# Taking x by quarters in the value product of a gated-MLP layer, with one x chunk turned on VectorE

## The chip, the core and the metric

The program runs on one core of a Trainium2 chip: TensorE (PE) multiplies, VectorE (DVE) and ScalarE (ACT) work elementwise, GpSimd (POOL) does little here, and SyncE (SP) issues the transfers that bring weights from memory. The metric is the device time of one execution in microseconds (us).

## What is computed

A two-layer encoder over 256 tokens of 2048 features, in float32. Layer 0 has the even mixer (spatial gating beside pooling), layer 1 an attention mixer; each is followed by a convolutional feed-forward block. The change lies in the beginning of the even mixer:

```python
h = rms_norm(x, norm_mix_g[i])
p = h @ w_in_even[e]                                  # 2048 -> 3072 columns: u, v, pool
z = jax.nn.gelu(p[..., :2 * A_WIDTH], approximate=False)
...
v = group_layer_norm(v, ln_g, ln_b)                   # v: columns 1024 to 2047 of p
w = jnp.where(block_causal_mask(A_BLOCK)[None], w_s, 0)
gate = jnp.einsum('gts,bnsgd->bntgd', w, v) + b_s...
y_a = u * gate
```

## The kernel before

**Pieces.** All weights come in pieces of 1 MB (128 partitions x 2048 floats), through a ring of four places (`RING`). SP issues the loads in a fixed order; the load of piece c waits until piece c - 4 has been split (`s_low`). ACT writes the rounded high part of a piece (`high`, L445), DVE the remainder (`low`, L821), and PE multiplies with both. `high` and `low` of piece c also wait until PE is through with piece c - 4 (`s_used`).

**Quads.** The values v are the first product: pieces 0 to 7, each a "quad" of four blocks of 128 features by 512 columns. A quad is 16 matmuls with the high part and 8 with the low part (`straight_quad`, L1369; `first_quad`, L1422 and L1427, for piece 0), and its sums stay in a PSUM bank pair of psA for its column half c. Before, column half 0 runs over the four quarters q of the features first (pieces 0 to 3), then column half 1 (pieces 4 to 7).

**Turning x.** The products need x with features on the partitions. x is taken in four chunks of 512 features. PE transposes a chunk against an identity (`transpose_x`, L1399, 8 matmuls) into PSUM; ACT multiplies by the gain and rounds (`turned_high`, L483, 4 instructions), DVE writes the remainder (`turned_low`, L845, 4 instructions), and then `s_turned` lets PE use the chunk. For the other norms DVE can do the turning instead (`turn_blocks`, L863: 16 block transposes into `xT`).

**The order of the work.** Each engine has one instruction stream, written by hand. On ACT and DVE, after a short prologue, a loop over n holds `high(n + 3)` or `low(n + 3)` and beside it what is listed for that n; what is behind a waiting instruction waits with it. Here "step n" is such a turn of the loop, and "quad n" is PE's n-th quad.

**Beside the quads.** ACT sums squares of x (`squares`), DVE makes 1/rms of each token (`mean_square`, `rstd_columns`, with ACT's `root` between them) and spreads it over rows (`spread_rstd`, L902). PE transposes small vectors, the taps of the convolutions and the spatial weights after quad 3 (L1452 to L1461). DVE copies them out (`spatial_weights`, L923 to L927) and signals `s_WT`. After quad 6 PE waits for `s_WT` and sums the spatial weights with a matmul against ones (L1465) into bank 0 of psT. DVE copies that sum (L998) and signals `s_wsr`, on which PE waits before the first pool product (`turned_half`, L1330), since that one writes banks 0 and 1 of psT. ACT's `gelu_v` (L517) reads the finished column halves from psA, at steps 3 and 7.

The order of PE around the quads, before:

```python
for c in range(2):
    for q in range(4):
        n = N_V0 + 4 * c + q
...
pe.wait_ge(s_wsr, 1)
```

Of the kernel before, what the change touches and what calls it, by code (L numbers as in the profile page):

```python
# [29 lines left out]
P = 128  # L30
RING = 4
LEAD = 3
# [17 lines left out]
def build(nc, x_in, norm_mix_g, norm_ffn_g, final_norm_g, w_in_even, ln_v_g, ln_v_b, w_spatial,  # L50
# [9 lines left out]
    AG = ln_v_g.shape[1]  # L60
# [4 lines left out]
    N_V0 = 0  # L65
# [35 lines left out]
    with ExitStack() as ctx:  # L101
# [169 lines left out]
        def turned_bank(s, n, kk):  # L271


            if s in (1, 3):
                return xT[n][:, kk, :]
            return psT[:, 2 * (n % 2) + kk // 2, TOK * (kk % 2):TOK * (kk % 2) + TOK]

        block = ctx.enter_context(nc.Block())
# [3 lines left out]
        def _(sp):  # L282
# [5 lines left out]
                sp.dma_start(raw[:, c % RING, :].rearrange("p (k n) -> p k n", k=kk), src)\  # L288
                    .then_inc(s_raw[c % RING], 16)

            for c in range(2):
                for q in range(4):
                    if c == 0 and q == 0:
                        piece0 = raw[:, 0, :].rearrange("p (k n) -> p k n", k=4)
                        src = quad(W_IN0, 0, 2)
                        sp.dma_start(x[:, :, 0:256], X_IN[:, :, 0:256]).then_inc(s_x_a, 16)
                        sp.dma_start(x[:, :, 256:512], X_IN[:, :, 256:512]).then_inc(s_x[0], 16)
                        sp.dma_start(piece0[:, 0:2, :], src[:, 0:2, :]).then_inc(s_raw_a, 16)
                        sp.dma_start(piece0[:, 2:4, :], src[:, 2:4, :]).then_inc(s_raw[0], 16)
                        continue  # L300
                    if c == 0:
                        sp.dma_start(x[:, :, 512 * q:512 * q + 512], X_IN[:, :, 512 * q:512 * q + 512])\
                            .then_inc(s_x[q], 16)
                    load(N_V0 + 4 * c + q, quad(W_IN0, q, 2 + c))
                if c == 0:

                    sp.dma_start(rows[32:64, :], norm_ffn_g.rearrange("l (m p) -> (l m) p", p=P)).then_inc(s_rows, 16)
                    sp.dma_start(rows[64:72, :], pool_scale[0].rearrange("(m p) -> m p", p=P)).then_inc(s_rows, 16)
                    sp.dma_start(rows[72:80, :], ln_v_g[0].rearrange("g (m p) -> (g m) p", p=P)).then_inc(s_rows, 16)
                    sp.dma_start(rows[80:88, :], ln_v_b[0].rearrange("g (m p) -> (g m) p", p=P)).then_inc(s_rows, 16)  # L310
                    for l in range(2):
                        sp.dma_start(conv_rows[:, l, 0:3, :], conv_w[l].rearrange("j (m p) -> m j p", p=P)).then_inc(s_conv, 16)
                        sp.dma_start(conv_rows[:, l, 3, :], conv_b[l].rearrange("(m p) -> m p", p=P)).then_inc(s_conv, 16)
                    sp.dma_start(w_sp, w_spatial[0].rearrange("g t s -> t g s")).then_inc(s_sp, 16)
                    sp.dma_start(bs, b_spatial[0:1, :, :].to_broadcast([P, AG, P])).then_inc(s_bs, 16)
            for j in range(4):
                for k in range(2):
                    load(N_POOL + 2 * j + k, half(W_IN0, k, 2 * AW + 256 * j))
# [106 lines left out]
        def _(a):  # L425
# [74 lines left out]
            a.wait_ge(s_raw[0], 16)  # L500
            a.activation(wh[:, 0, PIECE // 2:], raw[:, 0, PIECE // 2:], ACT.Copy).then_inc(s_high, 1)
            squares(0, 0)
            for n in range(1, 4):
                turned_high(0, n)
                if n < LEAD:
                    high(n)


            def gelu_v(c):

                a.wait_ge(s_used, N_V0 + 4 * c + 4)
                if c == 0:
                    a.wait_ge(s_rstd, 1)
                for t in range(2):
                    for g in range(2):
                        i = 4 * t + 2 * c + g
                        ins = a.activation(z[:, t, 512 * c + GD * g:512 * c + GD * g + GD],  # L517
                                           psA[:, 2 * c + t, GD * g:GD * g + GD], ACT.Gelu,
                                           scale=rstd[:, t:t + 1], accum_out=vsum[:, i:i + 1])
                fenced(ins, s_z, c + 1)  # L520
# [32 lines left out]
            for n in range(N_OUT0 + 16):  # L553
                k = n - N_OUT0
                if k in (6, 10, 14):
                    turned_high(1, k // 4 - 1)
                high(n + LEAD)
                if n < 2:
                    squares(0, n + 1)
                if n == 1:  # L560
                    squares(0, 3)
                if n == 1:
                    root(0)
                if n in (3, 7):
                    gelu_v(n // 4)
                if n in (8, 9):
                    z_squares(n - 8)
                if n == 10:
                    a.wait_ge(s_var, 1)
                    fenced(a.activation(vsd, vvar, ACT.Sqrt), s_zsd, 1)  # L570
                if N_POOL <= n < N_POOL + 8 and n % 2:
                    copy_low_half(Q_POOL + n // 2 - 4, (n // 2) % 2, n)
                if N_POOL + 2 <= n <= N_POOL + 8 and n % 2 == 0:
                    pooled_high(n // 2 - 5)
                if n == N_U[0][1]:
                    copy_low_half(Q_U[0], 0, n)
                if n in (N_WPOOL - 1, N_WPOOL):
                    for j in (0, 1) if n < N_WPOOL else (2, 3):
                        if j < 3:
                            a.wait_ge(s_wp, j + 1)  # L580
                        copy_low_half(Q_WPOOL + j, 0, n if j == 3 else None, bank=2 * (j % 2))
                    for j in (0, 1) if n < N_WPOOL else (2, 3):
                        yb_high(j)
                if n - 1 in N_GATE:
                    ya_high(N_GATE.index(n - 1))
                if n in N_GATE:
                    j = N_GATE.index(n)
                    if j:
                        copy_low_half(Q_U[j], j % 2, N_U[j][1])
                    gelu_u(j)  # L590
                if k >= 4 and k % 4 == 0:
                    squares(1, k // 4 - 1)
# [208 lines left out]
        def _(ve):  # L801
# [52 lines left out]

            def turn_blocks(s, n, tokens):


                for i in tokens:
                    for j in range(4):
                        src = x[32 * i:32 * i + 32, :, 512 * n:512 * n + 512]\  # L860
                            .rearrange("p t (k j b) -> p t k j b", k=4, j=4)[:, :, :, j, :]
                        dst = xT[n][32 * j:32 * j + 32, :, :].rearrange("p k (t i b) -> p t k i b", t=2, i=4)[:, :, :, i, :]
                        ins = ve.transpose(dst, src)  # L863
                if 3 in tokens:
                    ins.then_inc(s_turn, 1)
# [43 lines left out]

            ve.wait_ge(s_vec, 1)  # L910
            fenced(ve.tensor_copy(cols[:, 0:32], psA[:, 2, 0:32]), s_cols, 1)
            for n in range(4):
                turned_low(0, n)
                if n < LEAD:
                    low(n)

            def spatial_weights():

# [65 lines left out]
            for n in range(N_OUT0 + 16):  # L984
                k = n - N_OUT0
                if k in (6, 10, 14):
                    turned_low(1, k // 4 - 1)
                low(n + LEAD)
                if n == 1:
                    mean_square(0)  # L990
                    rstd_columns(0)
                if n == 4:
                    spatial_weights()
                if n == 5:
                    spread_rstd()
                if n == 6:
                    ve.wait_ge(s_wsum, 1)
                    fenced(ve.tensor_copy(WTsum, psT[:, 0, :].rearrange("p (g t) -> p g t", g=AG)), s_wsr, 1)  # L998
                    link(ve.memset(pp[:, :, 0:16], 0.0))
                    ve.wait_ge(s_bs, 16)  # L1000
                if n == 8:
# [306 lines left out]
        def _(pe):  # L1308
# [99 lines left out]
            def first_quad():  # L1408
# [3 lines left out]
                for kk in range(4):  # L1412
# [1 line left out]
                        pe.wait_ge(s_turned_a, 1)  # L1414
                        pe.wait_ge(s_high_a, 1)
                    if kk == 2:
                        transpose_x(0, 1)
                        pe.wait_ge(s_turned, 1)
                        pe.wait_ge(s_high, 1)
                    for t in range(2):  # L1420
# [14 lines left out]
            warm(5)  # L1435


            for c in range(2):
                for q in range(4):
                    n = N_V0 + 4 * c + q  # L1440
                    if n == 0:
                        first_quad()
                    else:
                        if c == 0:
                            pe.wait_ge(s_turned, q + 1)
                        straight_quad(n, c, H, 4 * q, q == 0, q == 3)
                    if n in (0, 1):
                        transpose_x(0, n + 2)
                    if n == 3:

                        pe.wait_ge(s_rows, 16 * 4)
                        pe.transpose(psT[:, 2, 8 * FT:8 * FT + 88], rows, ident[0:88, 0:88])  # L1452
# [9 lines left out]
                        ins.then_inc(s_spT, 1)  # L1462
                    if n == 6:
                        pe.wait_ge(s_WT, 1)
                        pe.matmul(psT[:, 0, :], ones[:, :], WT.rearrange("p g t -> p (g t)"), start=True, stop=True)\  # L1465
                            .then_inc(s_wsum, 1)
            pe.wait_ge(s_wsr, 1)
            for j in range(4):
                for k in range(2):
                    if j >= 2 and k == 0:  # L1470
                        pe.wait_ge(s_added, Q_POOL + j - 1)
                    turned_half(N_POOL + 2 * j + k, k, j % 2, H)
# [232 lines left out]
```

## Time and profile before

| | us |
|---|---|
| median of 3 runs | 2091.39 (2091.25 to 2091.41) |
| profiled execution, its own time | 2091.88 |
| span of the profiled execution | 2090.2 |
| PE busy | 2077.9 |
| DVE busy | 1577.1 |
| ACT busy | 1051.6 |

The time outside the span is 1.7 us. Times in the text count from the span's start. A matmul's duration in the trace overlaps its successor's, so the pace of PE is read from the starts of the weight loads (PEld), one for each matmul.

### The profile page before, as it was taken

To read this page: it belongs to the slowest core of one execution; us is meant where nothing else is said; L and a number is where in the kernel's file an instruction comes from. 1 tells how busy PE (TensorE), PEld (TensorE's weight loads), DVE (VectorE), ACT (ScalarE), POOL (GpSimd) and SP (SyncE) were. 2 spreads that over 40 slices of the span, in tenths; PEclk is the share of its full clock that TensorE was granted. 3 is DMA by queue.
4 is the path that set the end of the run, shared out by engine and by line. 5 is a ranking of instruction groups with operands and counts; after the bars stand their busy time and mean duration, and the time that the engine had idled before them with its cause. 6 is when DMAs were issued, how large, how long until landed. Compare 5 with 4: busy or idle time off the path is not lost.

```text
span 2090.2 us, 29731 instructions
## 1 busy us (share of the span) xinstructions
PE 2077.9 (99%) x10934; PEld 1793.5 (86%) x10934; DVE 1577.1 (75%) x2005; ACT 1051.6 (50%) x1095; POOL 25.4 (1%) x57
## 2 busy tenths in 40 slices
PE   9999999999999999999999999999999999999998
PEld 7888888888888888888888888888888888888886
DVE  6888886777676776776787788997776677767677
ACT  7554564445444444455554554465454444444454
POOL 0000000000000000000010000000000000000000
PEclk9999999999999999999999999999999999999999
DMA  8645565555555655554665565556555556556552
GB/s 300 201 164 200 181 204 199 182 200 182 192 191 182 208 190 181 195 190 147 204 206 163 191 208 175 175 184 212 195 185 189 194 184 204 181 181 200 181 198 105
DMA packets 317188, 397.17 MB, mean 190 GB/s; under 512 B 8612, under 2 KB 240844, under 8 KB 317004
## 3 DMA queue, kind: packets, MB, share of 16 engines
q1 hardware_dynamic: 313500, 391.27, 56.0%
q0 software_dynamic: 1056, 3.16, 0.8%
q10 hardware_dynamic: 2576, 1.98, 0.3%
q8 instruction: 36, 0.59, 0.1%
q14 instruction: 20, 0.16, 0.0%
HBM read 394.28 MB, written 2.11 MB: 190 GB/s over the span
## 4 chain that ended last, share of the span: by engine, by line
PE 96%; DVE 1%; SPq 1%; issue 1%; ACT 1%; DMA 0%; DVEq 0%; ACTq 0%
PE ps_turned L1330 37%; PE ps_straight L1369 33%; PE ps_turned L1339 20%; PE ps_straight L1330 1%; PE ps_turned L1369 1%; PE ps_straight L1339 1%; DVE w_low L821 0%; DMA w_raw<-in_w_in_even 0%; PE ps_straight L1604 0%; ACT w_high L445 0%; PE ps_straight L1614 0%; SPq L288 0%; PE ps_straight L1489 0%; PE ps_straight L1624 0%; PE ps_turned L1565 0%
## 5 line engine op out<-in xcount | busy, mean ns | idle before, releaser
L821 DVE TENSOR_TENSOR w_low<-w_raw,w_high 128x2048 fp32r<-128x2048 f32 x369 | 844.6, 2292 | 348.0 <-ACT w_high L445 314.1
L445 ACT ACTIVATE w_high<-w_raw 128x2048 fp32r<-128x2048 f32 x368 | 704.0, 1917 | 662.2 <-PE ps_straight L1369 286.7
L1330 PE MATMUL ps_turned<-h_split,w_high 128*128 128x512 f32 x3456 | 802.8, 390 | 0.9 <-DVE work L998 0.9
L1330 PEld LDWEIGHTS ps_turned<-h_split,w_high 128*128 128x128 f32 x3456 | 643.6, 188 | 131.8 <-DVE work L998 1.3
L1339 PEld LDWEIGHTS ps_turned<-h_split,w_low 128*128 128x128 f32 x3456 | 425.1, 192 | 6.1 <-DVE w_low L821 0.2
L1339 PE MATMUL ps_turned<-h_split,w_low 128*128 128x256 f32 x3456 | 428.9, 283 | 0.0
L1369 PE MATMUL ps_straight<-w_high,y_split 128*128 128x512 f32 x1792 | 425.5, 390 | 0.4 <-DVE x L872 0.4
L1369 PEld LDWEIGHTS ps_straight<-w_high,y_split 128*128 128x128 f32 x1792 | 335.9, 188 | 70.3 <-issue 0.8
L1369 PE MATMUL ps_straight<-w_low,y_split 128*128 128x512 f32 x896 | 221.3, 389 | 0.0
L1369 PEld LDWEIGHTS ps_straight<-w_low,y_split 128*128 128x128 f32 x896 | 168.2, 188 | 34.9
L1058 DVE SCALAR_TENSOR_TENSOR work<-work,conv_columns 128x256 f32<-128x256 f32 x352 | 154.4, 480 | 12.2 <-DVE work L1058 2.5
L872 DVE TENSOR_TENSOR x<-x,ps_straight 128x512 f32<-128x512 f32 x182 | 116.7, 682 | 54.4 <-PE ps_straight L1369 53.6
L603 ACT ACTIVATE work<-work,conv_columns 128x256 f32<-128x256 f32 x176 | 95.6, 590 | 60.0 <-DVE work L831 59.9
L454 ACT ACTIVATE work<-ps_turned 128x512 f32<-128x512 f32 x108 | 64.7, 599 | 92.8 <-PE ps_turned L1330 78.5
L827 DVE TENSOR_TENSOR work<-ps_turned,work 128x512 f32<-128x512 f32 x108 | 74.4, 689 | 27.9 <-ACT work L454 25.1
L1369 PE MATMUL ps_straight<-w_high,h_split 128*128 128x512 f32 x368 | 90.0, 397 | 0.0
L1369 PEld LDWEIGHTS ps_straight<-w_high,h_split 128*128 128x128 f32 x368 | 68.3, 188 | 14.2 <-issue 0.5
L1190 DVE STREAM_TRANSPOSE work<-work 32x96 f32<-32x96 f32 x256 | 69.1, 270 | 13.1 <-DVE small L1178 7.9
L831 DVE TENSOR_TENSOR work<-work,rstd_rows 128x512 f32<-128x512 f32 x103 | 71.3, 692 | 3.5
L863 DVE STREAM_TRANSPOSE work<-x 32x256 f32<-32x256 f32 x128 | 55.8, 436 | 2.0
L1369 PE MATMUL ps_straight<-w_low,h_split 128*128 128x512 f32 x184 | 45.5, 390 | 0.0
L1369 PEld LDWEIGHTS ps_straight<-w_low,h_split 128*128 128x128 f32 x184 | 34.5, 188 | 7.2
(186 smaller groups left out, 756.1 us busy)
## 6 DMA issues: line engine op xcount, KB each, us to landing
w_raw<-in_w_up SPq DMA_DIRECT2D x176, 1024.0 KB, 5.0
w_raw<-in_w_down SPq DMA_DIRECT2D x88, 1024.0 KB, 5.0
w_raw<-in_w_in_odd SPq DMA_DIRECT2D x48, 1024.0 KB, 5.5
w_raw<-in_w_in_even SPq DMA_DIRECT2D x23, 1024.0 KB, 5.3
w_raw<-in_w_out_even SPq DMA_DIRECT2D x16, 1024.0 KB, 4.9
w_raw<-in_w_out_odd SPq DMA_DIRECT2D x16, 1024.0 KB, 5.0
work<-c_rows POOLq DMA_DIRECT2D x8, 256.0 KB, 6.5
x<-in_x SPq DMA_DIRECT2D x3, 512.0 KB, 11.1
```

Of the source, the lines that this page charges most:

```text
L445: a.activation(wh[:, s, :], raw[:, s, :], ACT.Copy).then_inc(s_high, 1)
L454: fenced(a.activation(spare, src, ACT.Copy), s_spare, at(q + 1, 4, r))
L603: ins = a.activation(cc[j % 2][:, m, :], up[:, m, 2:], ACT.Identity, scale=taps[:, l, 2, bass.ds(i, 1)], bias=taps[:, l, 3, bass.ds(i, 1)])
L821: ve.tensor_tensor(wl[:, s, :], raw[:, s, :], wh[:, s, :].bitcast(F32), ALU.subtract).then_inc(s_low, 1)
L827: fenced(ve.tensor_tensor(to, src, spare, ALU.add), s_added, at(q + 1, 4, r))
L831: return ve.tensor_tensor(ap, ap, factor.unsqueeze(1).to_broadcast([P, 2, TOK]), ALU.mult)
L872: ins = ve.tensor_tensor(xc, xc, psA[:, 2 * (i % 2) + t, :] if sums is None else sums[:, t, :], ALU.add)
L1058: ins = ve.scalar_tensor_tensor(out=c[:, m, :], in0=up[:, m, 2 - back:TOK + 2 - back], scalar=taps[:, l, 2 - back, bass.ds(i, 1)], in1=c[: ...
L1190: ins = ve.transpose(dst, src)
L1330: ins = pe.matmul(ps[:, 2 * slot + m, :], hi[:, kk, P * m:P * m + P], acts[:, K, :], start=(K == 0 and not narrow_ran), stop=(K == KC - 1) ...
L1339: ins = pe.matmul(ps[:, 2 * slot + m, TOK:], lo[:, kk, P * m:P * m + P], acts[:, K, 0:TOK], start=(K == 0 and opens), stop=(K == KC - 1), ...
L1369: return pe.matmul(ps[:, 2 * slot + t, :], acts[:, k0 + kk, a0:a0 + P], weights[:, kk, :], start=begin, stop=end)
```

## The change

The eight quads run in another order: both column halves of a feature quarter one after the other (q outside, c inside), so that quad n uses x chunk n // 2. The loads follow: piece 1 comes before x chunk 1, and piece 3 before x chunk 3. Of x, PE transposes chunk 1 after quad 0 (it stood in the middle of quad 0) and chunk 2 after quad 2; chunk 3 is transposed by DVE in two halves, in steps 0 and 1, into `xT[0]`, and ACT and DVE split it in step 2. `squares(0, n + 1)` and `root` go with it to steps 0 to 2 and 3. DVE's `spread_rstd` moves from step 5 to 4, `spatial_weights` from 4 to 5, the copy of the spatial sums from 6 to 7; PE's small transposes move from behind quad 3 to behind quad 4. `gelu_v` moves to steps 6 and 7. The spatial sums go to bank 3 of psT, and PE waits for their copy ahead of the second pool panel (`j == 1`) instead of the first.

```diff
@@ SyncE
-            for c in range(2):
-                for q in range(4):
...
+            for q in range(1, 4):
+                if q == 1:
+                    load(N_V0 + 1, quad(W_IN0, 0, 3))
+                sp.dma_start(x[:, :, 512 * q:512 * q + 512], X_IN[:, :, 512 * q:512 * q + 512]).then_inc(s_x[q], 16)
+                if q < 3:
+                    load(N_V0 + 1 + q, quad(W_IN0, 1, 1 + q))
...
+            for q in (2, 3):
+                for c in range(2):
+                    load(N_V0 + 2 * q + c, quad(W_IN0, q, 2 + c))
@@ ScalarE
-            for n in range(1, 4):
+            for n in range(1, 3):
+                high(n)
                 turned_high(0, n)
-                if n < LEAD:
-                    high(n)
...
-                a.wait_ge(s_used, N_V0 + 4 * c + 4)
+                a.wait_ge(s_used, N_V0 + 7 + c)
...
                 high(n + LEAD)
-                if n < 2:
+                if n < 3:
                     squares(0, n + 1)
-                if n == 1:
-                    squares(0, 3)
-                if n == 1:
+                if n == 3:
                     root(0)
-                if n in (3, 7):
-                    gelu_v(n // 4)
+                if n == 2:
+                    turned_high(0, 3)
+                if n in (6, 7):
+                    gelu_v(n - 6)
@@ VectorE
-            for n in range(4):
-                turned_low(0, n)
-                if n < LEAD:
-                    low(n)
+            turned_low(0, 0)
+            for n in range(3):
+                low(n)
+                if n:
+                    turned_low(0, n)
...
+                if n == 2:
+                    turned_low(0, 3)
                 low(n + LEAD)
-                if n == 1:
+                if n < 2:
+                    turn_blocks(0, 3, (0, 1) if n == 0 else (2, 3))
+                if n == 3:
                     mean_square(0)
                     rstd_columns(0)
                 if n == 4:
+                    spread_rstd()
+                if n == 5:
                     spatial_weights()
-                if n == 5:
-                    spread_rstd()
-                if n == 6:
+                if n == 7:
                     ve.wait_ge(s_wsum, 1)
-                    fenced(ve.tensor_copy(WTsum, psT[:, 0, :].rearrange("p (g t) -> p g t", g=AG)), s_wsr, 1)
+                    fenced(ve.tensor_copy(WTsum, psT[:, 3, :].rearrange("p (g t) -> p g t", g=AG)), s_wsr, 1)
@@ TensorE
                     if kk == 2:
-                        transpose_x(0, 1)
                         pe.wait_ge(s_turned, 1)
...
-            for c in range(2):
-                for q in range(4):
-                    n = N_V0 + 4 * c + q
+            for q in range(4):
+                for c in range(2):
+                    n = N_V0 + 2 * q + c
...
-                    if n in (0, 1):
-                        transpose_x(0, n + 2)
-                    if n == 3:
+                    if n in (0, 2):
+                        transpose_x(0, n // 2 + 1)
+                    if n == 4:
...
-            pe.wait_ge(s_wsr, 1)
             for j in range(4):
                 for k in range(2):
+                    if j == 1 and k == 0:
+                        pe.wait_ge(s_wsr, 1)
```

PE, from the first quad on, before the change (L1422 and L1427 are quad 0, L1369 the later quads, L1399 the transposes of an x chunk, 8 matmuls each):

```order
L1422 MATMUL ps_straight<-w_high,h_split 128x512 x8
L1399 MATMUL ps_turned<-ident,x 128x128 x8
L1422 MATMUL ps_straight<-w_high,h_split 128x512 x8
L1427 MATMUL ps_straight<-w_low,h_split 128x512 x8
L1399 MATMUL ps_turned<-ident,x 128x128 x8
L1369 MATMUL ps_straight<-w_high,h_split 128x512 x16
L1369 MATMUL ps_straight<-w_low,h_split 128x512 x8
L1399 MATMUL ps_turned<-ident,x 128x128 x8
L1369 MATMUL ps_straight<-w_high,h_split 128x512 x16
```

The same stretch of PE in the changed kernel (its line numbers are 4 or 5 higher):

```order
L1426 MATMUL ps_straight<-w_high,h_split 128x512 x16
L1431 MATMUL ps_straight<-w_low,h_split 128x512 x8
L1404 MATMUL ps_turned<-ident,x 128x128 x8
L1374 MATMUL ps_straight<-w_high,h_split 128x512 x16
L1374 MATMUL ps_straight<-w_low,h_split 128x512 x8
L1374 MATMUL ps_straight<-w_high,h_split 128x512 x16
L1374 MATMUL ps_straight<-w_low,h_split 128x512 x8
L1404 MATMUL ps_turned<-ident,x 128x128 x8
L1374 MATMUL ps_straight<-w_high,h_split 128x512 x16
```

The transposes of chunk 2 now stand directly ahead of quad 3, and those of chunk 3 are gone from PE.

ACT before the change, from the squares of chunk 0 on (L467 is `squares`, L483 `turned_high`, L445 `high`):

```order
L467 ACTIVATE work,small<-x 128x512 x2
L483 ACTIVATE h_split<-ps_turned,feature_columns 128x256 x4
L445 ACTIVATE w_high<-w_raw 128x2048
L483 ACTIVATE h_split<-ps_turned,feature_columns 128x256 x4
L445 ACTIVATE w_high<-w_raw 128x2048
L483 ACTIVATE h_split<-ps_turned,feature_columns 128x256 x4
L445 ACTIVATE w_high<-w_raw 128x2048
```

The same stretch of ACT in the changed kernel (line numbers lower by one):

```order
L466 ACTIVATE work,small<-x 128x512 x2
L444 ACTIVATE w_high<-w_raw 128x2048
L482 ACTIVATE h_split<-ps_turned,feature_columns 128x256 x4
L444 ACTIVATE w_high<-w_raw 128x2048
L482 ACTIVATE h_split<-ps_turned,feature_columns 128x256 x4
L444 ACTIVATE w_high<-w_raw 128x2048
```

The three `high` in each are those of pieces 1, 2 and 3. Each stood behind the split of the x chunk of its own number; now it stands ahead of that split, and `high` of piece 3 directly behind that of chunk 2.

DVE before the change, from the `low` of pieces 5, 6 and 7 to the copy of the spatial sums:

```order
L821 TENSOR_TENSOR w_low<-w_raw,w_high 128x2048 x3
L923 COPY feature_columns<-ps_turned 128x56
L924 COPY conv_columns<-ps_turned 128x352 x2
L926 COPY work<-ps_turned 128x512
L927 MEMSET work 64x4x64
L821 TENSOR_TENSOR w_low<-w_raw,w_high 128x2048
L902 STREAM_TRANSPOSE rstd_rows<-small 32x2x32 x16
L821 TENSOR_TENSOR w_low<-w_raw,w_high 128x2048
L998 COPY work<-ps_turned 128x512
```

DVE in the changed kernel, first from the `low` of piece 3 (the first row) to those of pieces 5 and 6:

```order
L819 TENSOR_TENSOR w_low<-w_raw,w_high 128x2048
L863 STREAM_TRANSPOSE work<-x 32x2x4x32 x8
L819 TENSOR_TENSOR w_low<-w_raw,w_high 128x2048
L863 STREAM_TRANSPOSE work<-x 32x2x4x32 x8
L843 SCALAR_TENSOR_TENSOR h_split<-work,feature_columns,h_split 128x256 x4
L819 TENSOR_TENSOR w_low<-w_raw,w_high 128x2048 x2
L877 TENSOR_REDUCE small<-small 128x2
```

and then from the `low` of piece 7, which follows the last instruction of 1/rms (L886), to the copy of the spatial sums:

```order
L886 TENSOR_TENSOR small<-small 128x2
L819 TENSOR_TENSOR w_low<-w_raw,w_high 128x2048
L902 STREAM_TRANSPOSE rstd_rows<-small 32x2x32 x16
L819 TENSOR_TENSOR w_low<-w_raw,w_high 128x2048
L924 COPY feature_columns<-ps_turned 128x56
L925 COPY conv_columns<-ps_turned 128x352 x2
L927 COPY work<-ps_turned 128x512
L928 MEMSET work 64x4x64
L819 TENSOR_TENSOR w_low<-w_raw,w_high 128x2048 x2
L1003 COPY work<-ps_turned 128x512
```

The 16 block transposes, the spread of 1/rms and the `low` of piece 8 now stand ahead of the copies of the spatial weights (L924 to L928); before, there were no block transposes, and the other two stood behind.

## Rows read from the trace of the kernel before

**Rows 1.** The page, parts 1 and 4: busy time; the chain that ended last.

```profile
PE 2077.9 (99%) x10934; PEld 1793.5 (86%) x10934; DVE 1577.1 (75%) x2005; ACT 1051.6 (50%) x1095; POOL 25.4 (1%) x57
...
PE 96%; DVE 1%; SPq 1%; issue 1%; ACT 1%; DMA 0%; DVEq 0%; ACTq 0%
```

**Rows 2.** PE's waits in the whole run: total us, times, longest us.

```profile
PE ps_turned L1330 <- DVE work L998: 0.9, 1, 0.9
```

**Rows 3.** Timeline of PE's weight loads: start, us, line, operands, count, idle before.

```profile
8.90 1.69 PEld L1422 LDWEIGHTS ps_straight<-w_high,h_split 128*128 128x128 f32 x8 [0.98 <-DVE h_split L845]
11.09 0.86 PEld L1399 LDWEIGHTS ps_turned<-ident,x 128*128 128x128 f32 x8 [0.50 <-DMA x<-in_x]
...
13.65 1.77 PEld L1427 LDWEIGHTS ps_straight<-w_low,h_split 128*128 128x128 f32 x8
...
21.80 1.02 PEld L1399 LDWEIGHTS ps_turned<-ident,x 128*128 128x128 f32 x8
...
28.14 3.59 PEld L1369 LDWEIGHTS ps_straight<-w_high,h_split 128*128 128x128 f32 x16
...
33.58 0.14 PEld L1452 LDWEIGHTS ps_turned<-ident,work 88*128 88x128 f32 x1
...
34.82 3.51 PEld L1369 LDWEIGHTS ps_straight<-w_high,h_split 128*128 128x128 f32 x16
...
51.06 0.42 PEld L1465 LDWEIGHTS ps_turned<-work,ones 128*128 128x128 f32 x2
...
58.65 3.50 PEld L1330 LDWEIGHTS ps_turned<-h_split,w_high 128*128 128x128 f32 x16 [1.32 <-DVE work L998]
```

**Rows 4.** Timeline of ACT and DVE, up to 40 us.

```profile
9.43 1.06 ACT L501 ACTIVATE w_high<-w_raw 128x1024 fp32r<-128x1024 f32 x1 [1.57 <-DMA w_raw<-in_w_in_even]
...
10.59 2.29 DVE L821 TENSOR_TENSOR w_low<-w_raw,w_high 128x2048 fp32r<-128x2048 f32 x1 [0.89 <-ACT w_high L501]
...
14.03 1.92 ACT L445 ACTIVATE w_high<-w_raw 128x2048 fp32r<-128x2048 f32 x1
...
23.10 1.72 ACT L483 ACTIVATE h_split<-ps_turned,feature_columns 128x256 fp32r<-128x256 f32 x4 [2.67 <-PE ps_turned L1399]
...
23.98 1.75 DVE L845 SCALAR_TENSOR_TENSOR h_split<-ps_turned,feature_columns,h_split 128x256 fp32r<-128x256 f32 x4 [1.15 <-ACT h_split L483]
24.85 1.92 ACT L445 ACTIVATE w_high<-w_raw 128x2048 fp32r<-128x2048 f32 x1
...
33.88 0.16 DVE L877 TENSOR_REDUCE small<-small 128x2 f32<-128x8 f32 x1 [0.58 <-ACT work L467]
...
34.32 1.28 ACT L490 ACT_TABLE_LOAD   x1 [0.47 <-DVE small L878]
...
35.62 0.20 ACT L490 ACTIVATE small<-small 128x2 f32<-128x2 f32 x1
...
36.72 0.16 DVE L886 TENSOR_TENSOR small<-small 128x2 f32<-128x2 f32 x1
```

**Rows 5.** Timeline of DVE from 37 to 60 us.

```profile
37.86 4.49 DVE L821 TENSOR_TENSOR w_low<-w_raw,w_high 128x2048 fp32r<-128x2048 f32 x2 [0.98 <-ACT w_high L445]
...
47.02 0.21 DVE L923 COPY feature_columns<-ps_turned 128x56 f32<-128x56 f32 x1
...
49.18 0.27 DVE L927 MEMSET work<- 64x256 f32 x1
...
51.69 3.98 DVE L902 STREAM_TRANSPOSE rstd_rows<-small 32x64 f32<-32x64 f32 x16
```

**Rows 6.** Timeline of DVE near 180 us: half of a chunk turned for the next norm.

```profile
180.26 3.58 DVE L863 STREAM_TRANSPOSE work<-x 32x256 f32<-32x256 f32 x8
```

**Rows 7.** Windows of 1 us: busy of PE, PEld, DVE, ACT, POOL, then clock, DMA, GB/s.

```profile
2085.00:2086.00 1.00, 0.00 (x0) 0.00 (x0) 0.96 (x3) 0.76 (x1) 0.00 (x0) 0.86 0.00 0
2086.00:2087.00 1.00, 0.00 (x0) 0.00 (x0) 0.20 (x1) 0.17 (x1) 0.00 (x0) 0.50 0.40 146
```

**Rows 8.** Timeline of PE, its last matmuls.

```profile
2080.76 1.07 PE L1565 MATMUL ps_turned<-w_low,y_split 128*128 128x512 f32 x4
```

More of the change, by code:

```diff
@@ L271, in turned_bank @@
         def turned_bank(s, n, kk):
-            if s in (1, 3):
-                return xT[n][:, kk, :]
+            if s in (1, 3) or (s, n) == (0, 3):
+                return xT[n if s else 0][:, kk, :]
             return psT[:, 2 * (n % 2) + kk // 2, TOK * (kk % 2):TOK * (kk % 2) + TOK]
@@ L289, in load @@
                     .then_inc(s_raw[c % RING], 16)
-            for c in range(2):
-                for q in range(4):
[L293 to L315, printed above, removed]
@@ new lines, in _ @@
+            piece0 = raw[:, 0, :].rearrange("p (k n) -> p k n", k=4)
+            src = quad(W_IN0, 0, 2)
+            sp.dma_start(x[:, :, 0:256], X_IN[:, :, 0:256]).then_inc(s_x_a, 16)
+            sp.dma_start(x[:, :, 256:512], X_IN[:, :, 256:512]).then_inc(s_x[0], 16)
+            sp.dma_start(piece0[:, 0:2, :], src[:, 0:2, :]).then_inc(s_raw_a, 16)
+            sp.dma_start(piece0[:, 2:4, :], src[:, 2:4, :]).then_inc(s_raw[0], 16)
+            for q in range(1, 4):
[4 more added lines that the diff above has]
+                    load(N_V0 + 1 + q, quad(W_IN0, 1, 1 + q))
@@ new lines, in _ @@
+            sp.dma_start(rows[32:64, :], norm_ffn_g.rearrange("l (m p) -> (l m) p", p=P)).then_inc(s_rows, 16)
+            sp.dma_start(rows[64:72, :], pool_scale[0].rearrange("(m p) -> m p", p=P)).then_inc(s_rows, 16)
+            sp.dma_start(rows[72:80, :], ln_v_g[0].rearrange("g (m p) -> (g m) p", p=P)).then_inc(s_rows, 16)
+            sp.dma_start(rows[80:88, :], ln_v_b[0].rearrange("g (m p) -> (g m) p", p=P)).then_inc(s_rows, 16)
+            for l in range(2):
+                sp.dma_start(conv_rows[:, l, 0:3, :], conv_w[l].rearrange("j (m p) -> m j p", p=P)).then_inc(s_conv, 16)
+                sp.dma_start(conv_rows[:, l, 3, :], conv_b[l].rearrange("(m p) -> m p", p=P)).then_inc(s_conv, 16)
@@ L316, in _ @@
+            sp.dma_start(w_sp, w_spatial[0].rearrange("g t s -> t g s")).then_inc(s_sp, 16)
+            sp.dma_start(bs, b_spatial[0:1, :, :].to_broadcast([P, AG, P])).then_inc(s_bs, 16)
+            for q in (2, 3):
+                for c in range(2):
+                    load(N_V0 + 2 * q + c, quad(W_IN0, q, 2 + c))
             for j in range(4):
@@ L855, in turn_blocks @@
             def turn_blocks(s, n, tokens):
+                if s == 0:
+                    ve.wait_ge(s_x[n], 16)
                 for i in tokens:
@@ L861, in turn_blocks @@
                             .rearrange("p t (k j b) -> p t k j b", k=4, j=4)[:, :, :, j, :]
-                        dst = xT[n][32 * j:32 * j + 32, :, :].rearrange("p k (t i b) -> p t k i b", t=2, i=4)[:, :, :, i, :]
+                        dst = xT[n if s else 0][32 * j:32 * j + 32, :, :].rearrange("p k (t i b) -> p t k i b", t=2, i=4)[:, :, :, i, :]
                         ins = ve.transpose(dst, src)
@@ L1464, in _ @@
                         pe.wait_ge(s_WT, 1)
-                        pe.matmul(psT[:, 0, :], ones[:, :], WT.rearrange("p g t -> p (g t)"), start=True, stop=True)\
+                        pe.matmul(psT[:, 3, :], ones[:, :], WT.rearrange("p g t -> p (g t)"), start=True, stop=True)\
                             .then_inc(s_wsum, 1)
-            pe.wait_ge(s_wsr, 1)
             for j in range(4):
                 for k in range(2):
+                    if j == 1 and k == 0:
+                        pe.wait_ge(s_wsr, 1)
                     if j >= 2 and k == 0:
```

## The prediction

> **What bounds the kernel now.** I read the page's busy times and its chain first: PE is busy for 2077.9 of 2090.2 us and holds 96% of the chain that ended last [rows 1], so a time added to PE's stream, or a wait of PE, goes straight into the time. Next PE's waits: its longest after the first quad is 0.9 us, for the copy of the spatial sums [rows 2]; by the weight loads, which I count with, that gap is 1.32 us, and the other of note is 0.50 us for x chunk 1 [rows 3]. So the change can win little: those two gaps and the work it takes off PE. Then the timelines of PE, ACT and DVE over the first 60 us, for durations and for the order in which each stream goes.
>
> **What the change gives.** The 0.50 us for chunk 1 goes, since the transposes leave the middle of quad 0. The transposes of chunk 3 leave PE: 1.02 us [rows 3]. The 1.32 us before the pool product go, as the sums lie in another bank and the wait comes one panel later; between lie the 64 matmuls of the first panel, work enough to cover a copy that begins when it did before. Together **2.8 us**. The small transposes after a quad are moved, not added: 1.2 us (33.58 to 34.82) either way [rows 3]. The loads change places but carry the same bytes: before, chunk 1 and piece 1 had both landed when ACT cast piece 1 at 14.03 [rows 4], and PE needs the one at about 14.7 and the other at 15.7, so I cost that at nothing; were they 1 us late, it would be 1 us.
>
> **What it costs: four waits of PE.** I walk along the streams with durations of before. A quad is 5.44 us (28.14 to 33.58), its first 16 matmuls 3.6 of it [rows 3]; `high` 1.92, a first half of a chunk's ACT split 0.88 (DVE starts at 23.98 what ACT began at 23.10), the whole ACT split 1.75, the DVE split 1.75 [rows 4]; `low` 2.25 in a row (4.49 for two) [rows 5].
>
> First wait, quad 0. Its second half follows the first at 8.90 + 1.69 = 10.6 and ends at 12.3. `low` of piece 0 starts at 10.59, after ACT's 9.43 + 1.06, and takes 2.29 [rows 4]: PE waits until 12.9, **0.6 us**. The low part (1.8) ends at 14.7, the transposes of chunk 1 at 15.7. Quads 1 and 2 run to 26.6: their `high` come ahead of the chunk 1 split or right behind it, in time. The transposes of chunk 2 end at 27.6.
>
> Second wait, quad 3. It needs `high` of piece 3, which stands on ACT behind the split of chunk 2, and that split waits for the transposes that PE has only just made. ACT saw such transposes 0.3 us after their last weight load (21.80 + 1.02 to 23.10) [rows 3, 4]; then come 1.75 for the split, 1.92 for the cast and 0.1 to the next engine: quad 3 starts at 31.7, **4.0 us** late. Nothing covers this: no matmul is queued on PE between them. Before, quad 3's cast ended at 26.8 and PE came at 28.14 [rows 3, 4].
>
> Third wait, quad 5. `low` of piece 3 can start only now, at 31.7, and DVE has these in a row: `low` 2.25, 8 block transposes, `low` of piece 4, 8 block transposes. Eight of them on other rows of x took 3.58 [rows 6], 3.6 with a gap: DVE is through at 43.4. ACT then splits chunk 3's first half (0.9 with the handover), DVE its part (1.75), then `low` of piece 5: 48.35. PE meanwhile does quads 3 and 4 to 42.6, the small transposes to 43.8 and quad 5's first part to 47.4: **1.0 us** of waiting. Quad 6 ends at 55.7.
>
> Fourth wait, the spatial sums. PE needs DVE's copies of the spatial weights. DVE first finishes `low` of piece 6 (50.6), the mean square (0.4), waits for ACT's table load and root (34.32 to 35.82: 1.5) and makes 1/rms (1.06, to 36.88) [rows 4]. ACT's `high` of piece 7 stands behind that root: 52.5 + 1.95 = 54.5. Then DVE has `low` of piece 7 (56.8), the spread, 3.98 (60.8), `low` of piece 8 (63.0) and the copies, 47.02 to 49.45 = 2.43 [rows 5]: 65.5. PE got there at 55.7: **9.9 us**, with quad 7 and all pool products queued behind. Before, the copies were done at 49.45 and PE came at 51.06 [rows 3, 5], with 1.6 us to spare; 7.2 us of block transposes, 4.0 of spread, one more `low` and the late start of `low` 3 lie on the other side of that.
>
> Sum: 0.6 + 4.0 + 1.0 + 9.9 - 2.8 = **12.7 us** more. Later in the mixer nothing takes it back: PE is the bound there, and DVE and ACT are later by the same shift. Bounds: a handover here or there is overlapped, and the root's table load (1.28) might run before its wait instead of behind it as in [rows 4]: 11.3. With 0.1 us more at each of some dozen handovers: 13.7.
>
> **The clock.** After the last matmul (end 2081.8) the granted clock held at 1.00 and then fell to 0.50, the 1.2 GHz level; the mean of 0.86 in 2085 to 2086 puts the fall at 2085.7, 3.9 us after the end [rows 7, 8]. A wait of 9.9 us is far beyond that, so I expect quad 7 to begin at half speed. How soon the clock returns under work no row of before shows. Nothing, if at once; 5.9 us, if the sums (0.42 of weight loads [rows 3]) and the whole of quad 7 ran at half speed. I take 2.0: half of the 3.9 us which the fall took, if the return takes as long.
>
> The Trainium skill, TensorE: Matmul & The Clock Gate, Part 1, says that the throttled clock is the default and activity releases it, and that idleness brings it back. By that rule the fourth wait costs more than its length; without it the sum would stay at 12.7. The end of this trace agrees as far as the fall goes. The Trainium skill also speaks against the change in VectorE: DVE Perf Modes, Rules for kernel authors: it would have a 128x128 transpose on TensorE where PSUM may take it. The rows agree: 1.0 us of PE against 7.2 of DVE. Left on PE, by the sums above, the fourth wait would shrink to about 2.7 us.
>
> **Rivals.** (a) The same waits, but the clock holds or is back at once: 12.7 more, 2104.1. Against it are the last rows of the trace. (b) The clock falls in the second wait too: 4.0 us is about where it fell at the end. Another 2.0: 2108.2. Against it: PE's last matmul runs on for some tenths into that wait. (c) The other side: PE never waits. The copies would have to be done by 55.7, 9.8 us sooner than I find, for which DVE would have to have the block transposes (7.2) and a `low` in gaps of its stream. Its gaps in the walk, though, from 31.7 to 65.5, are the three short waits for ACT, 3.4 us in all. Then the 2.8 us are won: 2088.6, not slower, within 0.2%. (d) Only the first three waits are there, because the spatial weights come in time by something I misread: 5.6 - 2.8 = 2.8 more, 2094.2, also within 0.2%.
>
> **How the numbers follow.** The forecast is 12.7 + 2.0 = 14.7. On the profiled execution (2091.88, of which the span is 2090.2) that gives 2106.6, on the median of the runs, 0.5 lower, **2106.1**. Chances: forecast 0.70, (a) 0.12, (b) 0.10, (c) 0.05, (d) 0.03. The range takes in (a) and (b) and the bounds of the sum: from 2091.4 + 11.3 = 2102.7 to 2091.4 + 13.7 + 4.9 = 2110.0, the last term being most of the 5.9. About what a measurement of this kernel can tell from no change is 0.2%, 4.2 us. Slower by more: 0.92, the first three. Within: 0.07. Faster by more: 0.01, since the gains there are add up to 2.8 only.
>
> **What would show it.** In the profile after: a wait of PE for ACT's `high` of 4 us before quad 3; 1 us for `low` before quad 5; one near 10 us before the matmul of the spatial sums, released by DVE; the clock at 0.50 behind that; no wait of PE for the copy of the sums; DVE without a gap above 1.7 us between `low` of piece 3 and the copies. I'd be wrong if DVE's block transposes of x took much less than 3.6 us for eight, if ACT did not wait for chunk 2 ahead of piece 3, or if PE passed the spatial sums without a wait.

## The result, and the profile after

The changed kernel takes 2105.38 us in the median of six runs (2104.20 to 2106.55) against 2091.40 for the kernel before: 14.0 us slower, a ratio of 1.0066 with a 95% interval of 1.0056 to 1.0076. The profiled execution is the fastest of the six, 2104.20 us with a span of 2102.5, only 12.3 us more than the span of before; the lines below are of this execution.

PE's waits in the whole run (total us, times, longest us), which answer to [rows 2]:

```profile
PE ps_turned L1469 <- DVE work L928: 7.0, 1, 7.0
PE ps_straight L1374 <- ACT w_high L444: 3.7, 1, 3.7
...
PE ps_straight L1426 <- DVE w_high L850: 1.2, 1, 1.2
```

The wait for the copy of the spatial sums is gone. In its place stand a wait for DVE's spatial weights (the releaser L928 is the last instruction of `spatial_weights`) and one for ACT's cast of piece 3. The last row is the start of quad 0, as in [rows 3].

PE's weight loads in that stretch, as in [rows 3]:

```profile
8.37 3.52 PEld L1426 LDWEIGHTS ps_straight<-w_high,h_split 128*128 128x128 f32 x16 [1.31 <-DVE h_split L843]
12.19 1.69 PEld L1431 LDWEIGHTS ps_straight<-w_low,h_split 128*128 128x128 f32 x8 [0.30 <-DVE w_low L819]
...
25.69 1.02 PEld L1404 LDWEIGHTS ps_turned<-ident,x 128*128 128x128 f32 x8
30.69 5.92 PEld L1374 LDWEIGHTS ps_straight<-w_high,h_split 128*128 128x128 f32 x16 [3.98 <-ACT w_high L444]
...
45.17 3.51 PEld L1374 LDWEIGHTS ps_straight<-w_high,h_split 128*128 128x128 f32 x16
48.72 1.77 PEld L1374 LDWEIGHTS ps_straight<-w_low,h_split 128*128 128x128 f32 x8
...
63.34 0.50 PEld L1469 LDWEIGHTS ps_turned<-work,ones 128*128 128x128 f32 x2 [7.41 <-DVE work L928]
...
69.36 1.77 PEld L1374 LDWEIGHTS ps_straight<-w_low,h_split 128*128 128x128 f32 x8
71.17 3.59 PEld L1335 LDWEIGHTS ps_turned<-h_split,w_high 128*128 128x128 f32 x16
```

From the first quad to the first pool product PE needs 62.8 us (8.37 to 71.17) where it took 49.75 (8.90 to 58.65); as quad 0 began 0.5 us sooner, the pool products start 12.5 us later. The transposes of chunk 2 end at 26.7, and quad 3 starts 4 us later; its first 16 matmuls then take 5.9 us instead of 3.6. Quad 5's low part (48.72) follows without a wait. The spatial sums wait 7.41 us, and what follows them up to the pool products takes 7.8 us (63.34 to 71.17); the pool products follow at once.

The clock of the same execution, in windows of 1 us (busy of PE, PEld, DVE, ACT, POOL, then clock, DMA, GB/s):

```profile
28.00:29.00 1.00, 0.00 (x0) 0.00 (x0) 1.00 (x3) 0.97 (x3) 0.00 (x0) 1.00 1.05 387
29.00:30.00 1.00, 0.00 (x0) 0.00 (x0) 0.61 (x2) 1.00 (x1) 0.00 (x0) 0.56 1.06 391
...
35.00:36.00 1.00, 1.00 (x4) 0.72 (x4) 0.97 (x3) 0.97 (x3) 0.00 (x0) 0.53 0.94 346
...
59.00:60.00 1.00, 0.00 (x0) 0.00 (x0) 1.00 (x1) 0.97 (x3) 0.00 (x0) 0.92 0.18 54
60.00:61.00 1.00, 0.00 (x0) 0.00 (x0) 1.00 (x2) 1.00 (x1) 0.00 (x0) 0.50 0.00 0
...
66.00:67.00 1.00, 1.00 (x4) 0.78 (x3) 1.00 (x1) 0.00 (x0) 0.00 (x0) 0.67 0.30 27
67.00:68.00 1.00, 1.00 (x6) 0.79 (x6) 1.00 (x2) 0.00 (x0) 0.00 (x0) 1.00 0.83 260
```

It fell to 0.50 in both waits, and returned near 35.9 and 66.7.

The chain between the two waits, on ACT and DVE, answers to [rows 4 to 6]:

```profile
26.99 1.71 ACT L482 ACTIVATE h_split<-ps_turned,feature_columns 128x256 fp32r<-128x256 f32 x4 [8.12 <-PE ps_turned L1404]
28.73 1.91 ACT L444 ACTIVATE w_high<-w_raw 128x2048 fp32r<-128x2048 f32 x1
...
46.40 1.28 ACT L489 ACT_TABLE_LOAD   x1
50.19 0.20 ACT L489 ACTIVATE small<-small 128x2 f32<-128x2 f32 x1 [2.50 <-DVE small L878]
...
30.77 2.29 DVE L819 TENSOR_TENSOR w_low<-w_raw,w_high 128x2048 fp32r<-128x2048 f32 x1 [1.16 <-ACT w_high L444]
32.98 3.57 DVE L863 STREAM_TRANSPOSE work<-x 32x256 f32<-32x256 f32 x8
36.57 2.29 DVE L819 TENSOR_TENSOR w_low<-w_raw,w_high 128x2048 fp32r<-128x2048 f32 x1
38.89 3.59 DVE L863 STREAM_TRANSPOSE work<-x 32x256 f32<-32x256 f32 x8
43.52 1.83 DVE L843 SCALAR_TENSOR_TENSOR h_split<-work,feature_columns,h_split 128x256 fp32r<-128x256 f32 x4 [1.04 <-ACT h_split L482]
...
54.64 3.97 DVE L902 STREAM_TRANSPOSE rstd_rows<-small 32x64 f32<-32x64 f32 x16
58.65 2.29 DVE L819 TENSOR_TENSOR w_low<-w_raw,w_high 128x2048 fp32r<-128x2048 f32 x1
...
63.02 0.27 DVE L928 MEMSET work<- 64x256 f32 x1
```

ACT idles 8.12 us until PE has turned chunk 2; then DVE works from 30.77 to 63.29 with no gap above 1.1 us, and when it is through with the spatial weights PE goes on (63.34).

### The profile page after: what moved, and what is told of

Same layout as the page of the kernel before. It is cut to its first block, busy times and chain, and to the rows that moved or that the text cites. A ratio compares the mean times of both kernels' runs of the same rounds, so it can differ in the third digit from the quotient of the medians.

```text
span 2102.5 us, 29727 instructions
## 1 busy us (share of the span) xinstructions
PE 2080.4 (99%) x10926; PEld 1795.0 (85%) x10926; DVE 1584.5 (75%) x2021; ACT 1051.7 (50%) x1095; POOL 25.4 (1%) x57
## 3 DMA queue, kind: packets, MB, share of 16 engines
q1 hardware_dynamic: 313500, 391.27, 56.2%
## 4 chain that ended last, share of the span: by engine, by line
PE 98%; DVE 1%; ACT 0%; issue 0%; POOL 0%; DVEq 0%; ACTq 0%; POOLq 0%
PE ps_turned L1335 37%; PE ps_straight L1374 34%; PE ps_turned L1344 20%; PE ps_straight L1335 1%; PE ps_turned L1374 1%; PE ps_straight L1344 1%; DVE w_low L819 1%; DVE work L863 0%; PE ps_straight L1609 0%; PE ps_turned L1404 0%; PE ps_straight L1619 0%; PE ps_straight L1426 0%; ACT w_high L444 0%; PE ps_straight L1494 0%; PE ps_straight L1629 0%
## 5 line engine op out<-in xcount | busy, mean ns | idle before, releaser
L863 DVE STREAM_TRANSPOSE work<-x 32x256 f32<-32x256 f32 x144 | 62.8, 436 | 2.2
```

## The experiments

Two theories stood against each other. In the **sum of waits**, as in the prediction, each wait of PE adds to the time. In the **one chain**, only the path from the transposes of chunk 2 over ACT's split and cast and DVE's list to the spatial weights counts; whatever PE loses ahead of the fourth wait is hidden in it, and only the clock behind it is added. "The fourth wait" is the one ahead of the spatial sums, "the second" the one ahead of quad 3.

**The changed kernel again**, beside the next three on one chip.

> The changed kernel again, beside the next three on one chip, so that differences of 1 to 2 us between them can be read. Both theories: 2105.4, within 1.2 of it.

Measured: 2105.55 us (2104.74 to 2106.44); before, on that chip, 2091.15. Its profile differs from the first one where the clock had fallen: quad 3's first 16 matmuls took 5.1 us (5.9 there), and from the sums to the pool products it took 8.9 us (7.8 there).

```profile
30.87 5.09 PEld L1374 LDWEIGHTS ps_straight<-w_high,h_split 128*128 128x128 f32 x16 [3.98 <-ACT w_high L444]
...
63.51 0.50 PEld L1469 LDWEIGHTS ps_turned<-work,ones 128*128 128x128 f32 x2 [8.25 <-DVE work L928]
...
72.40 2.68 PEld L1335 LDWEIGHTS ps_turned<-h_split,w_high 128*128 128x128 f32 x12
```

**The cast of piece 3 ahead of the split of chunk 2.**

```diff
             for n in range(1, 3):
                 high(n)
+                if n == 2:
+                    high(3)
                 turned_high(0, n)
...
-                high(n + LEAD)
+                if n:
+                    high(n + LEAD)
```

> ACT casts piece 3 ahead of the split of x chunk 2 instead of behind it; nothing else changes. Theory of one chain (chunk 2 turned, split, cast of piece 3, DVE's list, spatial weights; what PE loses ahead of the fourth wait is hidden in it): quad 3 starts without its wait of 4.0 us and at full clock, but DVE's remainder of piece 3 starts only about 1.2 us sooner, behind the split of chunk 2, so the copies of the spatial weights are done 1.2 us sooner, the fourth wait grows from 7.4 to some 10 us, and the time is 2104.2. Theory of a sum of waits, as in the prediction: the 4.0 us and the 2.4 us that quad 3 lost to the clock are won, 2099.

Measured: 2104.62 us (2103.34 to 2105.17). PE's loads, and DVE's last copy of the spatial weights:

```profile
27.23 3.49 PEld L1377 LDWEIGHTS ps_straight<-w_high,h_split 128*128 128x128 f32 x16
32.54 1.69 PEld L1377 LDWEIGHTS ps_straight<-w_low,h_split 128*128 128x128 f32 x8 [1.82 <-DVE w_low L822]
...
47.16 1.97 PEld L1377 LDWEIGHTS ps_straight<-w_low,h_split 128*128 128x128 f32 x8 [2.33 <-DVE w_low L822]
...
62.76 0.50 PEld L1472 LDWEIGHTS ps_turned<-work,ones 128*128 128x128 f32 x2 [6.84 <-DVE work L931]
...
62.44 0.27 DVE L931 MEMSET work<- 64x256 f32 x1
```

The second wait is gone and quad 3 runs at full pace, yet the time falls by 0.9 us only, less than either kernel's own runs spread. PE now waits for `low` at quads 3, 4 (0.48) and 5 instead, and then for the same copies, which were done 0.7 us sooner than in the run beside it (62.71 against 63.45). So the second longest wait of the kernel was worth less than a quarter of its length. I expected the fourth wait to grow to some 10 us; it came to 6.8, since the waits for `low`, and a fall of the clock behind the longest of them, took the rest.

**PE kept busy in the fourth wait.**

```diff
+                        warm(28, psT[:, 1, 0:P])
                         pe.wait_ge(s_WT, 1)
```

`warm` multiplies the identity by ones; in this run and the next it takes the PSUM bank as a second argument. Each of its matmuls has two weight loads in the trace, so 28 of them show as x56.

> The changed kernel with 28 extra 128x128 matmuls of the identity by ones into an idle PSUM bank, ahead of the wait for the spatial weights: some 7 us of work in the wait of 7.4 us, so that PE isn't idle there. Clock theory: the clock stays at 1.00 through quad 7, which then takes 6.3 us from the sums to its end instead of 7.8; 1.5 us less, 2103.9, if the extra work doesn't outlast the wait. If the clock had nothing to do with it: 2105.4.

Measured: 2103.37 us (2102.64 to 2103.70), 2.2 less than the changed kernel beside it.

```profile
56.14 6.45 PEld L1411 LDWEIGHTS ps_turned<-ones,ident 128*128 128x128 f32 x56
64.36 0.30 PEld L1470 LDWEIGHTS ps_turned<-work,ones 128*128 128x128 f32 x2 [1.78 <-DVE work L928]
...
70.56 3.59 PEld L1335 LDWEIGHTS ps_turned<-h_split,w_high 128*128 128x128 f32 x16
```

The clock reads 1.00 throughout, and from the sums to the pool products PE takes 6.2 us (64.36 to 70.56) instead of 7.8. In the profile of the changed kernel on this chip that stretch took 8.9 us (63.51 to 72.40), so the low clock costs 1.6 in one execution and 2.7 in another; the 2.2 lies between.

**PE kept busy in the second wait.**

```diff
                     if n in (0, 2):
                         transpose_x(0, n // 2 + 1)
+                    if n == 2:
+                        warm(14, psT[:, 2, 0:P])
```

> The changed kernel with 14 extra 128x128 matmuls of the identity by ones into an idle PSUM bank behind the transposes of x chunk 2: some 3.5 us of work in the second wait of 4.0 us, so that quad 3 runs at full clock and is 2.4 us shorter. Theory of one chain: the copies of the spatial weights are done at the same time (63.3 us), the fourth wait grows by the 2.4 us less what the third wait takes, and the time stays at 2105.4 within 0.5. Theory of a sum of waits: 2.4 us less, 2103.

Measured: 2105.40 us (2104.32 to 2105.54), 0.15 less than the changed kernel beside it.

```profile
27.61 3.21 PEld L1411 LDWEIGHTS ps_turned<-ones,ident 128*128 128x128 f32 x28
31.62 3.50 PEld L1374 LDWEIGHTS ps_straight<-w_high,h_split 128*128 128x128 f32 x16 [0.81 <-ACT w_high L444]
...
48.66 1.69 PEld L1374 LDWEIGHTS ps_straight<-w_low,h_split 128*128 128x128 f32 x8 [1.50 <-DVE w_low L819]
...
64.27 0.50 PEld L1471 LDWEIGHTS ps_turned<-work,ones 128*128 128x128 f32 x2 [8.48 <-DVE work L928]
```

Quad 3 runs at full clock (3.5 us instead of 5.1 in the profile beside it, or 5.9 in the first), and nothing is won that can be measured: the third wait, absent in the changed kernel, is there with 1.5 us, and the fourth is 8.48 instead of 8.25. Both end with the same list of DVE. So what PE wins behind the transposes of chunk 2 comes back as waiting for that list, and what it loses there is hidden in it.

**Spatial weights ahead of the spread again** (steps 4 and 5 of DVE swapped back).

```diff
                 if n == 4:
-                    spread_rstd()
+                    spatial_weights()
                 if n == 5:
-                    spatial_weights()
+                    spread_rstd()
```

> The changed kernel with DVE's copies of the spatial weights back in step 4 and the spread of 1/rms in step 5. Theory of one chain: the spread (4.0 us) and the remainder of piece 8 (2.25) leave the chain, the copies are done at 57.1 instead of 63.3, the fourth wait shrinks from 7.4 to about 1.2 us, the clock doesn't fall in it, and the time is 6.2 + 1.5 lower: 2097.7. Theory that the late sums cost only what the clock takes, or that another wait takes the place: 2103.5 or more.

Measured: 2097.51 us (2096.43 to 2098.74). The copies end at 58.26, where I expected 57.1 (quad 0 began 0.85 us later than in the first profile of the changed kernel), PE's fourth wait is 1.22 us, and the clock holds at 1.00 behind it:

```profile
58.32 0.30 PEld L1469 LDWEIGHTS ps_turned<-work,ones 128*128 128x128 f32 x2 [1.22 <-DVE work L928]
...
64.51 3.59 PEld L1335 LDWEIGHTS ps_turned<-h_split,w_high 128*128 128x128 f32 x16
```

One swap of two steps takes away more than half of the loss.

**Chunk 2 turned behind quad 1.**

```diff
-                    if n in (0, 2):
-                        transpose_x(0, n // 2 + 1)
+                    if n in (0, 1):
+                        transpose_x(0, n + 1)
```

> The changed kernel with PE's transposes of x chunk 2 behind quad 1 instead of behind quad 2, so that ACT splits chunk 2 during quad 2. Theory of one chain: the second wait and its clock loss go, the chain starts 5.4 us sooner, the copies are done at about 57.9, and the time is 5.4 lower, 2100.0, with a fourth wait still of 7 to 8 us and a low clock behind it. Theory of a sum of waits: 4.0 + 2.4 lower, 2099.

Measured: 2100.10 us (2098.95 to 2100.64).

```profile
21.33 1.02 PEld L1404 LDWEIGHTS ps_turned<-ident,x 128*128 128x128 f32 x8
...
58.99 0.50 PEld L1469 LDWEIGHTS ps_turned<-work,ones 128*128 128x128 f32 x2 [8.45 <-DVE work L928]
```

No second wait: beside 0.56 us in quad 0, the one wait left in this stretch is the fourth, 8.45 us by the weight loads. From the transposes of chunk 2 to its end it is 37.7 us (21.33 to 58.99), as in the changed kernel (25.69 to 63.34): the chain began sooner by nearly one quad, and its length stayed.

**Chunk 3 turned by PE, right behind chunk 2** (no block transposes on DVE; the rest as changed).

```diff
                     if n in (0, 2):
                         transpose_x(0, n // 2 + 1)
+                    if n == 2:
+                        transpose_x(0, 3)
...
-                if n < 2:
-                    turn_blocks(0, 3, (0, 1) if n == 0 else (2, 3))
...
+                        pe.wait_ge(s_turned, 4)
                         pe.wait_ge(s_rows, 16 * 4)
```

> The changed kernel with x chunk 3 transposed by PE again, right behind chunk 2, so that DVE has no block transposes; the small transposes then also wait for the split of chunk 3. If the 7.2 us of block transposes lay wholly on the chain: the copies of the spatial weights 7.2 us sooner, 2098.3. Theory of one chain, walked through with ACT's list: the split of chunk 3 then waits for ACT's squares and casts, which end at about 39.6 instead of 43, so only 3.6 us of the 7.2 are won: 2101.9, with a fourth wait still of some 6 us.

Measured: 2101.55 us (2101.25 to 2102.50; before on that chip 2091.48). DVE's wait for the split of chunk 3, and the end of its copies:

```profile
40.40 1.75 DVE L843 SCALAR_TENSOR_TENSOR h_split<-ps_turned,feature_columns,h_split 128x256 fp32r<-128x256 f32 x4 [3.26 <-ACT h_split L482]
...
59.81 0.27 DVE L928 MEMSET work<- 64x256 f32 x1
```

Of the 7.2 us of block transposes about half were on the path: the time is 3.8 us below that of the changed kernel (2105.38). DVE waits 3.26 us for ACT, whose squares and casts stand ahead of that split. The fourth wait is 4.20 us, where I expected some 6.

**The new bank alone**, on the kernel before.

```diff
-            pe.wait_ge(s_wsr, 1)
             for j in range(4):
                 for k in range(2):
+                    if j == 1 and k == 0:
+                        pe.wait_ge(s_wsr, 1)
```

with `psT[:, 3, :]` for `psT[:, 0, :]` at the spatial sums and their copy.

> The kernel before with one part of the change alone: the spatial sums in bank 3 of psT, and PE's wait for their copy ahead of the second pool panel. Both theories: the wait of 1.32 us ahead of the first pool product goes and nothing takes its place, 2090.1. If it is paid back later in the mixer: 2091.4.

Measured: 2090.59 us (2090.30 to 2090.96, 11 runs) beside 2091.12 for before: ratio 0.9996, interval 0.9987 to 1.0005. The wait is gone from the trace, and the pool products start at 57.58, 1.1 us sooner than before; the 0.5 us between the medians is less than the 1.3 expected, and the measurement can't tell it from no change.

**The changed kernel with three steps moved**: chunk 2 behind quad 1, spatial weights in step 4 and spread in step 5 (both as above), and the spatial sums behind quad 7.

```diff
-                    if n == 6:
+                    if n == 7:
                         pe.wait_ge(s_WT, 1)
```

> The changed kernel with three steps in other places: the transposes of x chunk 2 behind quad 1, the copies of the spatial weights in step 4 and the spread in step 5, and the matmul of the spatial sums behind quad 7. Theory of one chain: DVE's list with the 16 block transposes is done at about 52 us, ahead of PE at the sums, no wait of PE above 0.6 us is left, and of the kernel before 0.5 + 1.0 + 1.3 - 0.5 us are won: 2089.0. If the block transposes on DVE cost PE in another way (a later remainder that is late): above 2091.4.

Measured: 2090.22 us (2089.90 to 2090.99, 11 runs) beside 2091.12: ratio 0.9996, interval 0.9987 to 1.0005. No wait is left in the value product, and the pool products start at 55.75, 2.9 us sooner than in [rows 3]. Further on PE has a wait that the kernel before had not:

```profile
PE ps_straight L1494 <- DVE w_low L819: 0.7, 1, 0.7
```

It is the pool weights' `low`: DVE's list there ends no sooner than it did (112.57 against 111.96 before), so a part of the gain is given back some 55 us later. This is the lowest median of all versions; that it beats the kernel before isn't shown at this precision.

**The same with chunk 3 turned by PE behind quad 3.**

```diff
-                    if n in (0, 1):
-                        transpose_x(0, n + 1)
+                    if n in (0, 1, 3):
+                        transpose_x(0, [1, 2, None, 3][n])
...
-                if n < 2:
-                    turn_blocks(0, 3, (0, 1) if n == 0 else (2, 3))
...
+                        pe.wait_ge(s_turned, 4)
                         pe.wait_ge(s_rows, 16 * 4)
```

> The best version so far, but with x chunk 3 transposed by PE behind quad 3 instead of by DVE: x by quarters with nothing turned on DVE. Theory of one chain: no wait of PE above 0.6 us in the value product; PE has 1.0 us more of work, some of which is won back ahead of the pool weights, where DVE was late by 0.7: 2090.5. If the order by quarters itself cost something: above 2091.4.

Measured: 2091.08 us (2090.40 to 2091.60, 11 runs) beside 2091.48: ratio 0.9997, interval 0.9988 to 1.0006. Beside 0.59 us in quad 0, PE has one wait in the value product, for the split of chunk 3 ahead of the small transposes: 0.7 us in the list of waits, 1.15 by the weight loads, where I expected none above 0.6. So the order by quarters costs nothing by itself that could be measured, and with three steps elsewhere nothing is left of the loss, whichever engine turns chunk 3. Whether DVE or PE should turn chunk 3 the two versions don't tell apart. The Trainium skill, VectorE: DVE Perf Modes, Rules for kernel authors, would have had PE do it; where DVE was on the chain it was right (3.8 us won by it), and where DVE had slack no run here bears it out.

## Why the prediction was right, step by step

**The direction and the size** (14.0 us against 14.7) came from the right mechanism: PE waits for the cast of piece 3, and then for spatial weights that stand behind a longer list on DVE. That the size came so near was in part luck. The two profiled executions are 12.3 us apart, 2.4 less than forecast, and the walk had put the end of the chain 2.2 us too late; the medians lie further apart, at 14.0, and in the changed kernel's second profile the low clock cost 2.7, more than the 2.0 that I had guessed for it.

**The gains** were there in the trace: no wait for chunk 1, no transposes of chunk 3 on PE, no wait before the pool products.

**The first wait** (0.6) measured 0.30; in the experiments' profiles it was 0.55 to 0.62 in seven and nothing in two.

**The second wait** (4.0) measured 3.98. But the clock fell in it, which I had as a rival that adds 2.0; it cost quad 3 2.3 us and, as the run with matmuls in that wait showed, added nothing.

**The third wait** (1.0) didn't appear, since quad 3 was slow; in the run whose extra matmuls held the clock in quad 3, it was 1.5.

**The fourth wait** (9.9) was 7.41. Its end was forecast at 65.5 and came at 63.3: the root's table load ran ahead of its wait (46.40, while the mean square came at 50.16), 1.3 us that I had as a bound and not in the sum; quad 0 began 0.5 sooner and its own wait was 0.3 shorter; handovers make up the rest. Its beginning came out nearly right (55.7 against 55.9) by luck: the slow quad 3 (2.3 us) made up for the missing third wait (1.0) and the earlier start.

**The clock behind it** (2.0) cost 1.6 in this execution and 2.7 in another.

**What was wrong in it.** Of the terms, the fourth wait was mis-sized by 2.5 us, half of that by the table load. And the waits were listed as if each were a price of its own. Their sum came out, because they were walked one after another and each was counted with what those ahead had left. But the fourth ends at a moment that PE's delays behind the transposes of chunk 2 didn't move, so rival (b) with its 2.0 on top was wrong: by the walk it would have come out at the forecast. The shorter sum is the moment at which PE passes the fourth wait, less the moment at which it came to the sums before, less the wait that goes, plus the clock behind it: 63.34 - 51.06 - 1.32 + 1.6 = 12.6, where the two spans differ by 12.3. In the same way it gives 5.9 for the swap of two steps, 9.1 for chunk 2 behind quad 1 and 9.4 for chunk 3 on PE, whose spans differ from that of before by 5.7, 8.8 and 9.5. The side estimate, that the fourth wait would shrink to 2.7 us with chunk 3 left on PE, took all 7.2 us of block transposes for time won; it measured 4.20, as ACT's list then came last.

## What to carry to other kernels

Where an engine waits several times on one chain of other engines, don't add the waits: find the moment at which the chain ends; a repair of an earlier wait is lost in the last one, as the cast of piece 3 showed (4.0 us removed, 0.9 won), unless it also starts the chain sooner, as the turning of chunk 2 behind quad 1 did (5.3 won). When work is handed from the busiest engine to one with idle time, ask what stands behind the new place in that engine's stream, and who waits for it: 1 us taken from PE put 7.2 us of DVE's work ahead of a result on which PE depended, and 3.8 of them were paid. A step for whose result the bounding engine waits next belongs ahead of one that is needed later (the swap of two steps won 7.9 us), and a consumer can also be moved later, as the spatial sums behind quad 7.

## What the runs showed of the hardware

The granted clock didn't fall after a fixed idle time. In the first profile of the changed kernel it fell 2.2 us after the last matmul in the second wait (26.95 to 29.1) and 3.5 after it in the fourth (56.36 to 59.8); at the end of the run before it was 3.9 us, and in the fourth wait of the run with the second wait filled 5.3 (56.2 to 61.5). Nor did it rise as soon as work was back: in the first profile it returned after 5.2 us of work in the one case (30.70 to 35.9) and 3.3 in the other (63.35 to 66.7), and behind the fourth wait of the second profile after 5.7 (63.51 to 69.2).

A fall can come after the wait, when PE is at work again. In the second profile of the changed kernel PE went on at 30.87 and the clock fell at 31.6. In the run with the cast moved a wait of 2.33 us by the weight loads (1.9 us without a matmul) ended at 47.16, and the clock fell between 48 and 49 us:

```profile
47.00:48.00 1.00, 0.84 (x4) 0.71 (x5) 1.00 (x2) 0.11 (x1) 0.00 (x0) 1.00 0.00 0
48.00:49.00 1.00, 1.00 (x5) 0.82 (x4) 1.00 (x1) 0.00 (x0) 0.00 (x0) 0.74 0.54 124
```

A wait of 1.22 us, in the run with two steps swapped, was followed by no fall. Whether the clock also makes the spread of the changed kernel's runs (2.3 us in six) is open: the kernel before spread by 1.1 us in six runs, but by 3.5 in 22 on another chip, with no such wait in its trace.
